# DMA transposes in place of TensorE transposes for ten norm blocks of a hybrid decoder step

## The reference, cut to what matters

```python
h = rms_norm(x) * (1 + sc1) + sh1            # first norm
proj = h @ w_in                              # q, f, i, g | B, C, h
o_rec  = hgrn2_chunked(q, k, logf, i, s_rec) # 4 heads, normed, gated
o_conv = gb * short_conv(gc * hv, s_conv, w_conv)
x = x + g1 * (concat(o_rec, o_conv) @ w_out)
h2 = rms_norm(x) * (1 + sc2) + sh2           # second norm
x = x + g2 * (square(relu(h2 @ w_up)) @ w_down)
y = rms_norm(x) * g_final
```

## Time and profile before

| | us |
|---|---|
| median of 3 runs | 860.02 |
| lowest, highest | 856.55, 861.51 |
| the profiled execution | 856.58 |
| its span on the slowest core (2) | 855.0 |
| spans of all cores | 854.0 to 855.0 |

### The profile page before, as it was taken

One profiled execution on the slowest core, in us unless ns is written; L12 is line 12 of the kernel. 1 busy time (PEld: TensorE's weight loads), 2 busy tenths in 40 slices (PEclk: granted clock), 3 DMA queues, 4 the chain that ended last, 5 costly groups with the idle time before them and its releaser, 6 DMA issues.

```text
span 855.0 us, 16507 instructions; the slowest of 8 cores (854.0 to 855.0 us)
## 1 busy us (share of the span) xinstructions
PE 809.3 (95%) x5896; PEld 514.2 (60%) x5945; DVE 452.5 (53%) x876; ACT 368.1 (43%) x803; POOL 174.1 (20%) x231
## 2 busy tenths in 40 slices
PE   1589999999999999999999999999999999999996
PEld 1458776587876868656545654564456445644864
DVE  2367996376787867943016553455345535541522
ACT  3258963364666778447404322332233213310412
POOL 3110243254125232410012012101110111111002
PEclk9999999999999999999999999999999999999999
DMA  8999935988993349699996225213421332113001
GB/s 150 192 197 188 189 109 96 199 216 190 217 196 127 122 148 164 150 174 186 189 200 201 94 55 155 99 50 65 149 96 50 78 108 74 38 38 99 26 1 50
DMA packets 38957, 109.57 MB, mean 128 GB/s; under 512 B 15030, under 2 KB 16054, under 8 KB 33884
## 3 DMA queue, kind: packets, MB, share of 16 engines
q0 software_dynamic: 6624, 44.14, 30.9%
q1 hardware_dynamic: 30524, 58.34, 22.5%
q10 hardware_dynamic: 1728, 6.03, 2.2%
HBM read 123.93 MB, written 22.68 MB: 171 GB/s over the span
## 4 chain that ended last, share of the span: by engine, by line
PE 90%; DMA 5%; ACT 2%; issue 2%; DVE 1%; POOL 0%; ACTq 0%; DVEq 0%; POOLq 0%
PE B L511 89%; DMA adaf<-w_ada 5%; PE B L522 1%; ACT W L538 1%; ACT kt L538 0%; POOL mix L545 0%; ACT sq L538 0%; ACT Sb L538 0%; DVE W L545 0%; POOL xn L575 0%; ACT WX L538 0%; DVE W L549 0%; ACT xn L538 0%; POOL cB L575 0%; DVE sm L545 0%
## 5 line engine op out<-in xcount | busy, mean ns | idle before, releaser
L511 PE MATMUL B<-h2T,wup 128*128 128x384 bf16 (+1 forms) x1536 | 240.2, 317 | 0.0
L511 PE MATMUL B<-wdn,uT 128*128 128x512 bf16 (+1 forms) x1098 | 233.7, 373 | 1.2
L511 PEld LDWEIGHTS B<-h2T,wup 128*128 128x128 bf16 x1536 | 149.5, 98 | 83.8
L511 PE MATMUL B<-hT,win 128*128 128x256 bf16 (+1 forms) x1728 | 193.8, 269 | 5.6 <-DMA win<-w_in 5.0
L538 ACT ACTIVATE W<-B 128x384 f32<-128x384 f32 (+2 forms) x209 | 103.8, 498 | 201.3 <-PE B L511 180.9
L511 PEld LDWEIGHTS B<-wdn,uT 128*128 128x128 bf16 x1120 | 109.6, 98 | 124.8
L511 PEld LDWEIGHTS B<-hT,win 128*128 128x128 bf16 x1728 | 158.9, 98 | 26.8 <-issue 6.1
L545 POOL TENSOR_TENSOR xr<-xr,W 128x512 f32<-128x512 f32 x63 | 82.6, 1317 | 283.8 <-DVE W L545 256.9
L545 DVE TENSOR_TENSOR uT<-W,B 128x384 bf16<-128x384 f32 (+1 forms) x160 | 83.7, 525 | 80.7 <-ACT W L538 75.2
L545 DVE TENSOR_TENSOR W<-B,Gp 128x512 f32<-128x512 f32 (+1 forms) x65 | 44.2, 680 | 154.3 <-PE B L511 154.1
L538 ACT ACTIVATE W<-xr 128x1024 bf16<-128x1024 f32 (+2 forms) x19 | 18.3, 965 | 134.3 <-POOL xr L545 129.8
(11 more groups left out here) (159 smaller groups left out, 664.2 us busy)
## 6 DMA issues: line engine op xcount, KB each, us to landing
x<-xr SPq DMA_DIRECT2D x17, 512.0 KB, 12.2
xn<-x SPq DMA_DIRECT2D x17, 512.0 KB, 6.2
xr<-x SPq DMA_DIRECT2D x17, 512.0 KB, 5.2
ada<-w_ada POOLq DMA_DIRECT2D x8, 1024.0 KB, 15.2
xr<-xp SPq DMA_DIRECT2D x16, 512.0 KB, 7.7
wup<-w_up POOLq DMA_DIRECT2D x8, 1024.0 KB, 14.5
wdn<-w_down POOLq DMA_DIRECT2D x8, 1024.0 KB, 40.5
yp<-xr SPq DMA_DIRECT2D x15, 512.0 KB, 2.6
```

The lines of the kernel that those rows point to most:

```text
L511: ins = e.matmul(o_, lhsT=l_, rhs=r_, start=st, stop=sp_, skip_group_check=True)
```

## The change

It does ten blocks' transposes by DMA in place of TensorE: in `sample_mod`, so for the sample's first and its second norm (both call it); in `norm1` for prompt tiles 5, 6 and 7, two blocks each; and in `norm2` for blocks 0 and 1, by `cross`. The DMA writes the normed block straight into `hT` or `h2T0`, and scale and shift follow in place: eight `ts` a prompt tile or block, and for the sample four `tensor_tensor` as before, reading SBUF where they read PSUM. The transposes' outputs have marks of their own (`#d0`, `#d1`), each with its own semaphore, since two of them now write the two halves of one `hT`. What the older DMA transposes write is marked in the same way. The three blocks of group 1 keep TensorE's transposes, as do prompt tiles 0 to 4.

```diff
-            key = eng + ((":in:" + writes[0][0].name) if (...) else (":out:" + reads[0][0].name))
+            key = eng + ((":in:" + writes[0][0].name + writes[0][1]) if (...) else (":out:" + reads[0][0].name))
...
     def sample_mod(nbv, nbn, dst, dst_n, c0, j_sh, j_sc, spare=None):
-        M, Mn = NR.take()
-        Mb = M[:, :].bitcast(BF16)
-        tr([(Mb[:, j * 128:(j + 1) * 128], nbv[:, j * 128:(j + 1) * 128], ident) for j in range(8)], [nbn, "cB"], [Mn])
+        turn(dst[:, :, c0:c0 + 128], nbv, [nbn], [dst_n + "#d0"], 128 * 2048)
...
-            tt("dve", tmv, trv, scb, ALU.mult, [Mn, "modT%d#%d" % (j_sc // 8, jh)], [Wn])
-            tt("dve", hv, tmv, shb, ALU.add, [Wn, "modT%d#%d" % (j_sh // 8, jh)], ["%s#%d" % (dst_n, jh)])
+            tt("dve", tmv, hv, scb, ALU.mult, [dst_n + "#d0", "modT%d#%d" % (j_sc // 8, jh)], [Wn])
+            tt("dve", hv, tmv, shb, ALU.add, [Wn, dst_n + "#d0", "modT%d#%d" % (j_sh // 8, jh)], ["%s#%d" % (dst_n, jh)])
...
+        if ti >= 5:
+            for b in range(2):
+                turn(h[:, :, b * 128:(b + 1) * 128], nbs[b][0], [nbs[b][1]], ["%s#d%d" % (hn, b)], 128 * 2048)
+            for jj in range(8):
+                ts("dve", h[:, jj, :], h[:, jj, :], modT[:, 8 + jj, 0:1], modT[:, jj, 0:1], ALU.mult, ALU.add,
+                   [hn + "#d0", hn + "#d1", "modT0#%d" % (jj // 4), "modT1#%d" % (jj // 4)], ["%s#%d" % (hn, jj)])
+            return h, hn
...
-                norm2(bgroups[0][n_ - 5:n_ - 4], None, "h2T0_", n_ - 5)
+                norm2(bgroups[0][n_ - 5:n_ - 4], None, "h2T0_", n_ - 5, cross=n_ - 5 < 2)
```

More of the change, by code:

```diff
@@ L147, in op @@
         if dma is not None:
-            key = eng + ((":in:" + writes[0][0].name) if (writes and (writes[0][0].rng is not None or not reads)) else (":out:" + reads[0][0].name))
+            key = eng + ((":in:" + writes[0][0].name + writes[0][1]) if (writes and (writes[0][0].rng is not None or not reads)) else (":out:" + reads[0][0].name))
             o.chan = key
@@ L880, in sample_mod @@
     def sample_mod(nbv, nbn, dst, dst_n, c0, j_sh, j_sc, spare=None):
-        M, Mn = NR.take()
-        Mb = M[:, :].bitcast(BF16)
-        tr([(Mb[:, j * 128:(j + 1) * 128], nbv[:, j * 128:(j + 1) * 128], ident) for j in range(8)], [nbn, "cB"], [Mn])
+        turn(dst[:, :, c0:c0 + 128], nbv, [nbn], [dst_n + "#d0"], 128 * 2048)
         for jh in range(2):
             W, Wn = (spare[0][:, jh * 512:(jh + 1) * 512], "%s#%d" % (spare[1], jh)) if spare else WT.take()
-            trv = Mb[:, jh * 512:(jh + 1) * 512].rearrange("p (j s t) -> p j s t", s=16, t=8)
             tmv = W[:].rearrange("p (j s t) -> p j s t", s=16, t=8)
@@ L1227, in norm2 @@
                 hn = pre + "%d" % s
-                turn(dst, nbv, [nbn], [hn], 128 * 2048)
+                turn(dst, nbv, [nbn], [hn + "#d0"], 128 * 2048)
                 for j in range(8):
                     ts("dve", dst[:, j, :], dst[:, j, :], modT[:, 24 + j, 0:1], modT[:, 16 + j, 0:1], ALU.mult, ALU.add,
-                       ["%s#%d" % (hn, j), "modT2#%d" % (j // 4), "modT3#%d" % (j // 4)], ["%s#%d" % (hn, j)])
+                       [hn + "#d0", "modT2#%d" % (j // 4), "modT3#%d" % (j // 4)], ["%s#%d" % (hn, j)])
                 continue
```

## The result

The changed kernel takes 887.99 us (878.08 to 897.35, four runs) against 858.42 of the kernel before on the same chip: ratio 1.0312, 95% interval 1.0273 to 1.035. It is slower by 3.1%; the forecast was 859.0, the range 853.5 to 865. What the profile shows of the cores isn't particular to it: in the three others the cores' spans lie 28, 22 and 33 us apart.

The account below looks back on a forecast made before the run. TensorE, busy 95% of the span, was taken to bound the kernel. The terms -4.5 - 0.6 + 4.5 = -0.6, or -1 with the weights ending earlier, took 860.0 to 859.0 us; range 853.5 to 865.

Parts of the forecast that it names:

- price of the late landing, +4.5: Tile 5's transposes land at 256.5 to 257.5 behind weight loads; TensorE waits 4.5 us, bounds 0 and 9.
- rival 1: Tile 5's transposes land by 250, ahead of xr or in bulk; all of -5.1 stays, 854.9; chance 0.25.
- test (b): Landings: 3 to 4 us for tiles 6, 7 and group 0; over 25 for tile 5, ending just after wup1's load.
- Test (c): TensorE idle 3 to 6 us before tile 5's first projection, DVE about as long before its first hT<-hT.
- queueing model: Beside weights, two queues alternate packet for packet whatever their size: 1.3 packets a us per queue and engine, 48 us a block.
- rival 3: DVE and ACT stand still before tile 5's landing; TensorE waits 9 to 10 us; 865; chance 0.18.
- rival 2: Tile 5's transpose packets pass in groups of 16; both blocks land at 255, TensorE waits 3 us; 858; chance 0.13.
- -4.5 for TensorE's instructions: Ten blocks' transposes taken from TensorE, 0.45 us each, shorten the kernel by 4.5 us.
- Test (a): TensorE's transposes from W number 104 in place of 184, with 10 more DMA transposes, 21.
- (d): No idle time from late landings before tiles 6 and 7 or the up part at 364.
- -0.6 for the sample's second norm: At about 346, the norm leaves DVE early by DMA; 0.6 us gained, bounds 0 and 1.4.
- rival 4: The planner orders everything anew, other steps move by a us or two either way; 860; chance 0.08.

Follow-up runs that it names:

- e3: Changed kernel with tile 5's two transposes replaced by plain copies in the same 256-byte packets and queue places; ratio 1.0056.
- e2: Kernel before with only tile 5's first norm transposed by DMA; ratio 1.0363, from two executions.
- e4: Kernel before with the second norms of the second channel-mixer group's three blocks by DMA, beside the down-weight loads; ratio 1.0298.
- e6: Kernel before with only the first norms of tiles 6 and 7 by DMA (four blocks); ratio 0.9990.
- e7: Kernel before with only group 0's blocks 0 and 1 by DMA; ratio 0.9990.
- e9: Kernel before with the first norms of tiles 6 and 7 and group 0's blocks 0 and 1 by DMA; ratio 0.9995.
- e5: Changed kernel with DMA transposes and POOL's weight loads made to wait for each other, sample's second norm on TensorE; ratio 1.0055.
- e10: Kernel before with tiles 6 and 7, group 0's blocks 0 and 1 and the sample's second norm by DMA; ratio 1.0010.
- e8: Kernel before with only the sample's two norms by DMA; ratio 1.0053.
- e13: Kernel before with tile 5's first norm alone by DMA, and St0, St1, wup0, wup1 loaded one at a time; 863.05 us, ratio 1.0063.
- e11: Changed kernel with St0, St1, wup0, wup1 each issued only after the last one's landing; 867.2 us, one execution that counts.
- m4 (d): Transfer stages without the kernel, engines idle: 4 transposes and 4 weight loads, two loads in flight; 79 GB/s in one window on core 1.
- kind (c): Transfer stages without the kernel, engines idle: 8 transposes and 4 loads, all issued when the first transpose has landed; 169 GB/s in one window.
- m3 (g): Transfer stages without the kernel, engines busy: 2 plain copies in place of transposes, 4 weight loads, at most two in flight; stage time not given.
- m1: Row of transfer stages without the kernel, of transposes, loads, copies and stores alone or together; 8 transposes of 128x1024 alone took 12.7 us on core 1.

## Why the prediction was wrong

**The step that failed is the price of the late landing, +4.5.** The prediction said that no row has a transpose beside POOL's queue, and then bounded it from rows of 1 KB copies: late, but harmless to the weights, which "end up to a us earlier". That is what copies do (e3). With transposes the weights themselves stood, 54.1 us in place of 14.4, and with them whatever else goes by DMA. The bounds of 0 and 9 us were bounds of the mechanism that I had in mind, not of the cost that I didn't know.

**The transposes' place in the queue was wrong.** The prediction had them begin at 246, when `xr`, `xn` and `convs` had landed. SP's queue in the changed kernel, core 5:

```profile
217.65 9.37 SPq L571 DMA_TRANSPOSE hT<-W  x2
227.12 0.48 SPq L575 DMA_DIRECT2D gates<-xr  x1
227.69 0.82 SPq L575 DMA_DIRECT2D xr<-xp  x2
```

They stand ahead of `xr`, which is what rival 1 asked for, and landed at 228 and 234; DVE took them up at 249.2 without waiting. By test (b) ("an end before 250 proves me wrong") the forecast fails on cores 5 and 2 even without a long jam: there the 4.5 us are nothing. In the changed kernel no core shows the price as the prediction worked it out.

**The place of the wait was wrong too.** Test (c) looked for idle time before tile 5's first projection. In the changed kernel that is 2.3 us on core 7, 0.9 on core 1 and nothing on the others; what stops core 7's TensorE is `St` (5.1 us) and its own instructions (19.8). Neither stands in the diff. I had looked up who waits for the moved transfer, and not what else uses the same engines. In e2, where tile 5 alone is moved, the wait does stand where it was looked for, 7.3 to 25.1 us on seven of the eight cores, as long as the jam makes it.

**The queueing model was right, and rival 3 with it, elsewhere.** One packet for one: 708 against 713 in e4, so rival 2's groups don't occur. DVE standing still before the landing: 46 us there. Rival 3's way was the result there, with 23.5 us of waiting and not 10.

**-4.5 for TensorE's instructions held as a count, not as time.** Test (a), groups by shape, and the transposes that SP issued, of the changed kernel:

```profile
L522 PE MATMUL B<-cB,W 128*128 128x128 bf16 x104 | 9.0, 234 | 12.7 <-DVE W L549 12.6
...
h2T<-W SPq DMA_TRANSPOSE x14, 3.3
hT<-W SPq DMA_TRANSPOSE x7, 4.0
```

104 in place of 184, and 21 DMA transposes. But their time came back in part only: e6 and e7 gained about 0.9 us each by the ratio, for 1.8 and 0.9 forecast, and e9, which is both, 0.4 for 2.7. The changed kernel itself can't show it. The landings of tiles 6 and 7 and group 0 took 3.0 to 6.8 us on all cores, where test (b) said 3 to 4; no wait came of it, so (d) holds.

**-0.6 for the sample's second norm did not.** The wait at 346 gave way to two, here on core 5 with the wait before tile 4's last out-projection ahead of them:

```profile
272.56 2.72 PE L511 MATMUL B<-wout,mix 128*128 128x512 bf16 x6 [4.25 <-POOL mix L545]
...
348.15 0.38 PE L511 MATMUL B<-sm,vt 128*128 128x128 bf16 x4 [0.83 <-DVE sm L545]
348.97 7.07 PE L511 MATMUL B<-wout,mix 128*128 128x512 bf16 x32 [0.31 <-ACT st L538]
```

1.43 us became 1.14, and 4.25 us came in elsewhere, which by e5 and e10 belongs to the sample's first norm. That is rival 4, the new order; I had given it 860 with 8 in 100, and the sample's two norms alone cost 0.5% (e8). Even a core without a jam gained nothing: core 5 ended at 856.4, the longest of before at 855.0.

## What to carry to other kernels

Before a transfer is put beside others, look for a row in which this very kind of transfer runs beside that very kind of queue; where there is none, the price is unknown on the side of the neighbours too, and they include the instruction queues. With DMA transposes, keep the bulk loads around them apart (e5), or issue one after the landing of the other (e13; rare jams, e11); all at once was clean in the stages, but wasn't tried in the kernel. What jammed most was two loads in flight and a new one at each landing. Check by the landing times of the loads and by the spans of all cores, not by the transposes alone. And where a planner orders the work, a gain of a few tenths of a us per edit can't be counted on: the order's scatter here was 0.1 to 0.5%.

## What the runs showed of the hardware

- DMA transposes with another queue's loads two in flight: packets of 8 KB stood open for up to 16.2 us, packets of 256 bytes for up to 4.0, in 24 of 24 stages (m4 (d)), and core 1's traffic fell from 169 GB/s in a stage of kind (c) to 79; with plain copies in the same packets of 256 bytes none stood over 3 us (m3 (g)).
- TensorE can run dry for want of instructions: 19.8 us on core 7, while q8 brought nothing from 218.9 to 264.9. The profile calls it "issue". The Trainium skill's page "Runtime: NRT & Kernel Launch", section "Instruction fetch mechanics", calls the cost of crossing a 16 KiB block "mostly hidden"; it is in the kernel before (0.2 us of "issue" on core 2 in the whole span), and isn't while DMA engines stand.
- Two queues share an engine packet for packet, 8 KB against 256 bytes (708 to 713), so a queue of short packets beside weights got 1.5 packets a us on each engine with 256 bytes each, and 1.3 with 1 KB each.
- A transpose of 128 x 1024 by itself lands in 3.2 to 3.6 us, and eight in a row take 12.7 us (m1).
